# Moving conditioning chunks between a decoder's seams and its dense stages, and regrouping the norm sums

## The reference, cut to what matters

```
m = (silu(c) @ cond_w + cond_b).reshape(c.shape[0], N_COND, 1, D_MODEL)   # cond_w: 1024 x 9216 a layer
def pre(i, h):  return rmsnorm(h, norm_pre[i]) * (1.0 + m[:, 3 * i + 1]) + m[:, 3 * i]
def post(i, h, y, rw): return h + rw * m[:, 3 * i + 2] * rmsnorm(y, norm_post[i])
x = post(0, x, swiglu(pre(0, x), ffn_w_in[0], ffn_w_out[0]), 0.5)
x = post(1, x, mixer(pre(1, x), ...), 1.0)
x = post(2, x, swiglu(pre(2, x), ffn_w_in[1], ffn_w_out[1]), 0.5)
```

## Time and profile before

| what | value |
|---|---|
| runs | 1388.15, 1389.68, 1395.26 us, median 1389.68 |
| profiled execution | 1388.44 us, span 1386.7 us |
| granted TensorE clock, mean | 0.988 |
| TensorE busy | 1327.9 us, 96% of the span |
| VectorE, ScalarE, GpSimd busy | 58%, 42%, 5% |
| DMA | 324.49 MB, mean 234 GB/s |

### The profile page before, as it was taken

One profiled execution on the slowest core, in us unless ns is written; L12 is line 12 of the kernel. 1 busy time (PEld: TensorE's weight loads), 2 busy tenths in 40 slices (PEclk: granted clock), 3 DMA queues, 4 the chain that ended last, 5 costly groups with the idle time before them and its releaser, 6 DMA issues.

```text
span 1386.7 us, 34431 instructions
## 1 busy us (share of the span) xinstructions
PE 1327.9 (96%) x13990; PEld 1268.5 (91%) x13990; DVE 805.6 (58%) x1178; ACT 586.7 (42%) x965; POOL 64.6 (5%) x141
## 2 busy tenths in 40 slices
PE   6899999999989999999999999999998998999997
PEld 5899999999966899999989999998997687999997
DVE  2555553668894655554465555446789657555544
ACT  2532333443565543333363333345337555333442
POOL 4000000110020000000000000002001000000000
PEclk9999999999999999999999999999999999999999
DMA  9878779789989895568876557987997993655552
GB/s 330 262 231 258 218 243 311 224 252 335 293 257 343 266 312 152 155 179 270 261 232 173 157 167 224 291 259 213 315 333 209 331 325 92 171 163 160 145 161 84
DMA packets 423815, 324.49 MB, mean 234 GB/s; under 512 B 15559, under 2 KB 351719, under 8 KB 423696
## 3 DMA queue, kind: packets, MB, share of 16 engines
q1 hardware_dynamic: 421124, 317.03, 75.3%
q0 software_dynamic: 2272, 5.61, 1.3%
q10 hardware_dynamic: 300, 0.13, 0.0%
HBM read 317.93 MB, written 4.78 MB: 233 GB/s over the span
## 4 chain that ended last, share of the span: by engine, by line
PE 87%; DVE 5%; DMA 3%; SPq 2%; ACT 1%; DVEq 1%; issue 1%; POOL 0%; ACTq 0%
PE PS L604 24%; PE PS L605 23%; PE PS L606 23%; PE PS L632 4%; PE PS L666 2%; PE PS L910 2%; PE PS L667 2%; PE PS L668 2%; PE PS L956 1%; SPq L486 1%; DMA direct<-in_cache_sb_v 1%; DMA raw<-in_ffn_w_in 1%; SPq L453 1%; DVE sm L2000 1%; PE PS L676 1%
## 5 line engine op out<-in xcount | busy, mean ns | idle before, releaser
L1702 DVE TENSOR_TENSOR w_lo<-raw,w_hi 128x1024 fp32r<-128x1024 f32 (+1 forms) x368 | 392.9, 1106 | 446.8 <-ACT w_hi L1315 446.3
L1315 ACT ACTIVATE w_hi<-raw 128x1024 fp32r<-128x1024 f32 (+1 forms) x368 | 337.7, 960 | 657.1 <-PE PS L606 576.5
L604 PE MATMUL PS<-a_hi,w_hi 128*128 128x288 f32 x1760 | 524.1, 298 | 0.4 <-issue 0.4
L605 PE MATMUL PS<-a_lo,w_hi 128*128 128x288 f32 x1760 | 519.2, 295 | 0.0
L606 PE MATMUL PS<-a_hi,w_lo 128*128 128x288 f32 x1760 | 517.5, 294 | 0.0
L604 PEld LDWEIGHTS PS<-a_hi,w_hi 128*128 128x128 f32 x1760 | 329.8, 187 | 3.8 <-issue 3.5
L606 PEld LDWEIGHTS PS<-a_hi,w_lo 128*128 128x128 f32 x1760 | 331.4, 188 | 0.0
L605 PEld LDWEIGHTS PS<-a_lo,w_hi 128*128 128x128 f32 x1760 | 330.4, 188 | 0.7 <-issue 0.5
L605 PE MATMUL PS<-h_lo,w_hi 128*128 128x288 f32 x704 | 208.4, 296 | 0.0
L604 PE MATMUL PS<-h_hi,w_hi 128*128 128x288 f32 x704 | 208.1, 296 | 0.0
L606 PE MATMUL PS<-h_hi,w_lo 128*128 128x288 f32 x704 | 208.0, 296 | 0.0
(11 more groups left out here) (324 smaller groups left out, 1159.4 us busy)
## 6 DMA issues: line engine op xcount, KB each, us to landing
raw<-in_ffn_w_in SPq DMA_DIRECT2D x176, 512.0 KB, 5.0
direct<-in_cond_w SPq DMA_DIRECT2D x240, 256.0 KB, 5.0
direct<-in_cache_sb_k SPq DMA_DIRECT2D x128, 256.0 KB, 4.3
direct<-in_cache_sb_v SPq DMA_DIRECT2D x128, 256.0 KB, 4.6
raw<-in_ffn_w_out SPq DMA_DIRECT2D x64, 384.0 KB, 3.8
raw<-in_mix_w_in SPq DMA_DIRECT2D x48, 512.0 KB, 7.1
raw<-in_ffn_w_out SPq DMA_DIRECT2D x64, 320.0 KB, 4.5
side<-in_cond_w SPq DMA_DIRECT2D x48, 256.0 KB, 5.3
```

The costliest lines, as they stand in the source:

```text
L604: pe.matmul(out, whi, hi, start=begins and i == 0, stop=False)
L605: pe.matmul(out, whi, lo, start=False, stop=False)
L1315: act.activation(w_hi[:, s, at_:at_ + n], raw[:, s, at_:at_ + n], ACT.Copy)\
L1702: tt(w_lo[:, s, at_:at_ + n], raw[:, s, at_:at_ + n], w_hi[:, s, at_:at_ + n], ALU.subtract).then_inc(lo_done.sem, 1)
```

## The change

Five edits, and the DMAs that belong to them:

- In `group(1)` of the first feed-forward's output part, TensorE does all four chunks of third 0 behind output step 5, where it did two.
- SyncE loads slots 2 and 3 of third 2 inside the output part (`i == 2`, next to output steps 10 and 11) and no longer between the mixer's input loads.
- `mixer_seam` holds eight chunks, where it held ten; the sums of pairs 1 to 3 stand in one run, then a chunk, then `spread_x` and two chunks, where it was three.
- `layer_seam` puts a chunk ahead of pair 0, one behind it, the sums of pairs 1 to 3 in one run, a chunk, then `spread_x`.
- The third seam of layer 0 ends with two chunks (numbers 4 and 5), where it was three (4 to 6); chunk 6 goes ahead of chunks 7 to 9 behind input step 2 of the second feed-forward.

```diff
--- before.py
+++ after.py
@@ -515,7 +515,7 @@
                             if l + n and s == 2:
                                 sp.wait_ge(ss_out.sem, ss_out.at(l + n, 0) * 32)
                             cond_side(lc, x, s)
-                        if i == 2 and s < 2 and n == 0:
+                        if i == 2 and s < 4 and n == 0:
                             cond_part(lc, x, 2, s)
                         if i == 2 and s >= 2:
                             sp.wait_ge(w_used.sem, w_used.at(l, POS_IN[n] + N_IN))
@@ -553,8 +553,6 @@
                         mix(l, mix_w_in, POS_MI, j, j % 2, MIX_STEPS[j][1])
 
                 mix_in(0, 1)
-                for s in range(2, 4):
-                    cond_part(l, 2, 2, s)
                 mix_in(2, 3)
                 key_chunks(l, 0, 1)
                 mix_in(4)
@@ -747,7 +745,7 @@
                             for slot in (2, 3):
                                 part_chunk(l, 1, 2, slot)
                         elif s % 3 == 2 and n == 1 and not final:
-                            for c in ((7, 8, 9), (10, 11))[s // 3]:
+                            for c in ((6, 7, 8, 9), (10, 11))[s // 3]:
                                 cond_chunk(l, *cond_in, *divmod(c, 4))
                     with pe.Fori(3, NCH // 2 + 3) as i:
                         for s in range(2):
@@ -774,15 +772,15 @@
                         if first and s == 1:
                             pe.wait_ge(h_ready.sem, h_ready.at(l, (n + 1) * N_IN))
                         out_chunk(l, n, i * 4 + s, s)
-                        if s < chunks and s % 2 == 1:
+                        if chunks and s == 1:
                             pe.wait_ge(mod_ready.sem, mod_ready.at(l, 1))
-                            for slot in (s - 1, s):
+                            for slot in range(chunks):
                                 part_chunk(l, 2, 0, slot)
 
                 NG = N_OUT // 4
                 group(0, True)
                 if n == 0:
-                    group(1, chunks=2)
+                    group(1, chunks=4)
                 with pe.Fori(2 if n == 0 else 1, NG - 1) as i:
                     group(i)
                 group(NG - 1)
@@ -817,20 +815,17 @@
 
             def mixer_seam(l):
 
-                part_chunk(l, 2, 0, 2)
+                side_chunk(l, 2, 0)
                 spread_y(l, 0)
-                part_chunk(l, 2, 0, 3)
-                side_chunk(l, 2, 0)
-                side_chunk(l, 2, 1)
+                for slot in range(1, 4):
+                    side_chunk(l, 2, slot)
                 pair_squares(l, 0, 0)
-                side_chunk(l, 2, 2)
-                pair_squares(l, 0, 1)
-                side_chunk(l, 2, 3)
-                pair_squares(l, 0, 2)
                 part_chunk(l, 2, 2, 0)
-                pair_squares(l, 0, 3)
+                for j in range(1, KP):
+                    pair_squares(l, 0, j)
+                part_chunk(l, 2, 2, 1)
                 spread_x(l, 1)
-                for slot in range(1, 4):
+                for slot in range(2, 4):
                     part_chunk(l, 2, 2, slot)
 
             def layer_seam(l):
@@ -840,10 +835,12 @@
                 spread_y(l, 2)
                 for slot in range(1, 4):
                     part_chunk(l + 1, 1, 0, slot)
-                for j in range(KP - 1):
+                side_chunk(l + 1, 1, 0)
+                pair_squares(l, 2, 0)
+                side_chunk(l + 1, 1, 1)
+                for j in range(1, KP):
                     pair_squares(l, 2, j)
-                    side_chunk(l + 1, 1, j)
-                pair_squares(l, 2, KP - 1)
+                side_chunk(l + 1, 1, 2)
                 spread_x(l + 1, 0)
                 side_chunk(l + 1, 1, 3)
                 for slot in range(2):
@@ -1281,7 +1278,7 @@
                 for h in range(2):
                     last = column_sums(5, ysq[:, 2 * ((N_MO - 1) % 2) + h, :], False, h == 1)
                 last.then_inc(ssy_done.sem, 1)
-                filled_seam(l, 1, 2, DP_C[0], 0, 4 if l + 1 < L else 1, 7 if l + 1 < L else 4, l)
+                filled_seam(l, 1, 2, DP_C[0], 0, 4 if l + 1 < L else 1, 6 if l + 1 < L else 4, l)
                 ffn(l, 1, (2, DP_C[0]))
                 if l + 1 < L:
                     layer_seam(l)
```

## The result

The changed kernel takes 1402.83 us (median of 6 runs, 1399.27 to 1407.84); the kernel before, beside it on the same chip, takes 1389.59. The ratio is 1.0098, with a 95% interval of 1.0076 to 1.0119: slower by 13 us. The forecast was 1393.0 with a range up to 1400, so the time is outside the range.

What follows compares the result with a forecast made beforehand. It took one long TensorE stream (87% of the chain) as the bound. Seams -7.5, chunks +4.70, stalls +6.8 gave +4.0 on 1388.44, so 1392.4; half of 1.24 added gave 1393.0, own range 1389 to 1396.5, wider range 1386 to 1400.

Steps and rivals of the forecast that it cites:

- The stall before step 12: First feed-forward's output part: two early chunk loads delay step 12's weights, TensorE stands 3.4 us per layer, 6.8 in all.
- The clock behind the stall: Rival: stalls at output step 12 bring half-clock products, 1.6 to 3 us per layer, giving 1396.2 to 1399; chance 0.20.
- the wait of 2.59 in the third seam: Layer 0's third seam: chunk waits 2.59 for its DMA, next step takes usual time; cited against the lowered-clock rival.
- The standstill of layer 0's mixer seam: The 1.47 standstill behind the spread would come ahead of it, unhidden; bounds 0 and 1.47, 0.50 taken.
- DMA is quieter there now, and I take 0.50: Layer 0's mixer seam: reason given for costing the standstill ahead of the spread at 0.50.
- The layer seam: Seam between the layers: 0.97 from sums in one run and 0.18 from fewer chunks, less 0.55 for its standstill.
- ends when something arrives, whatever I reorder: Layer seam: standstill ends at 719.54 regardless of order; bounds 0 and 1.15, 0.55 taken.
- the third seam: Layer 0's third seam: fewer chunks behind the spread cut its distance to the next step from 12.48 to 10.75, 1.73.
- layer 1's mixer seam: Sums in one run give 1.33 and fewer chunks behind the spread 2.65.
- the chunks: Chunks moved to dense stages: two more behind output step 5 per layer, chunk 6 behind input step 2; 4.70 added.
- the reload behind chunk 6: Second feed-forward: later slot reload delays input step 5's weights some 4 us; costed at nothing, 1 to 2 if uncovered.
- The floor of 10.75 from spread to next step: Seams: third input pair ready 7.51 behind the spread, plus half a step of 3.24; nothing gets below 10.75.

Runs made afterwards that it cites:

- late_loads: Changed kernel with the loads of third 2's slots 2 and 3 issued behind the weights of output steps 12 and 13; 1390.66 us, ratio 1.0013.
- stall_filled: Changed kernel plus 64 matmuls with unused sums, turned over four column groups, ahead of output step 12; 1399.54 us, ratio 1.0074.
- one_load: Changed kernel with slot 2's load kept early and slot 3's moved behind step 12's weights; 1396.71 us, ratio 1.0049, runs 1390.1 to 1398.32.
- late_pad: late_loads plus 40 full-width matmuls added at TensorE's start, before the first products; 1402.03 us, one run.
- late_shift: late_loads plus 80 matmuls into one group of 32 columns ahead of the first products; 1401.98 us, ratio 1.0083.
- late_fill160: late_loads plus 80 matmuls (160 in the trace) over four column groups ahead of the first products; 1387.78 us, ratio 0.9990.
- nine_fill80: nine_chunks plus 40 matmuls (80 in the trace) over four column groups ahead of the first products; 1385.98 us, ratio 0.9979.
- nine_chunks: Changed kernel with three chunks behind output step 5, nine in the mixer seam, slot 2's load behind step 12's weights, slot 3's at its old place; 1387.70 us, ratio 0.9986.

## Why the prediction was wrong

**The stall before step 12: right, with a margin misread.** The step "the weights of step 12 land 6.1 later, 0.86 to spare, 1.88 given by the chunks: 3.4 us" measured 3.20 and 4.21. In late_loads, with those bytes elsewhere, it was 0; with half of them 0.55 to 0.85. The margin was smaller than 0.86: the row at 249.66 is the split of step 13, which waits for step 11's last product, and in the trace of the kernel before step 12 itself begins at 249.47.

```profile
249.47 0.29 PE L604 MATMUL PS<-h_hi,w_hi 128*128 128x288 f32 x1
```

The low half was ready at 248.80, so 0.67 is left. In layer 1 the same split begins at 917.35 and step 12 at 918.97; with 0.96 for the split that leaves 0.66. So the margin does not tell the layers apart. The weights do: counted from the start of the output part, their split begins 5.6 later in layer 0 and 6.6 in layer 1, on both sides of the 6.1, and from issue to split they take 8.2 and 9.4, where both took 7.4 to 7.6 before. Why they took 1.2 longer in layer 1 is not shown.

**The clock behind the stall: the step that failed.** The forecast's sum has no term for it. It stood among the rivals with 0.20 and in the forecast at nothing, because the wait of 2.59 in the third seam was followed by a step of the usual length. It came in both layers. The price was 1.6 each, the low end of the rival's 1.6 to 3. stall_filled shows that it is the idle time that brings it: the same late weights, TensorE busy, whole clock. One wait without a loss was no proof against it. 0.55 to 0.85 (one_load) cost no clock, 3.20 and 4.21 did, but between them the length alone does not decide: the clock stayed at 1.00 behind the wait of 2.59 in the kernel before and behind the standstill of 2.14 in the changed one, and fell behind the 2.00 in the earlier trace rows and, in late_loads, behind the 1.43 that ends at 947.80:

```profile
948.00:950.00 2.00, 2.00 (x72) 2.00 (x68) 1.01 (x1) 0.08 (x1) 2.00 (x4) 0.55 0.17 19
```

What else decides there no run shows. With the two half clocks the forecast would have been 1396.2, still 6.6 short.

**The standstill of layer 0's mixer seam: right place, wrong size, and a second one.** The prediction said that it would come ahead of the spread, at the same place in the program. It did, 79 records from the seam's end before and after; and the place 128 records ahead of it, at 207, where the kernel before shows no gap, now has one too. The term that was mis-sized, and its reason, is "DMA is quieter there now, and I take 0.50": the two lasted 2.14 and 1.06. The windows around the first one show that there was no DMA traffic to speak of:

```profile
281.00:283.00 2.00, 0.35 (x13) 0.08 (x1) 1.93 (x3) 1.91 (x4) 1.42 (x2) 1.00 0.00 0
283.00:285.00 2.00, 1.50 (x67) 1.50 (x70) 1.91 (x4) 1.42 (x3) 0.35 (x1) 1.00 0.00 0
```

A DMA share of 0.00 and a standstill of 2.14: the length does not come from contention. The seam cost 0.77 where 1.21 was to be gained, a miss of 2.0. late_pad, late_shift and late_fill160 show that the places go by the count of instructions. In their profiles the three seams take 2.0 to 2.9 less than in late_loads, and in nine_fill80's 2.4 less than in nine_chunks; the times of late_fill160 and nine_fill80 lean the same way, with overlapping intervals.

**What the standstills are.** The last DMA traffic ahead of the standstill of 2.14 is one packet of 16 KB on the queue that the profile calls instruction; it starts at 280.88, 2.62 before TensorE goes on at 283.50. The DMA view of the changed kernel from 280.75 to 281:

```profile
q8 instruction: 1, 0.02, 28.3%
```

The 17 traces hold 70 standstills of 0.35 or more that the profile puts down to "issue", and 68 of them end 2.2 to 2.9 after the start of such a packet, whether DMA moves 398 GB/s meanwhile or nothing. (The other two, of 0.42 and 0.38, lie in the mixer.) So TensorE goes on some 2.5 after the packet starts, and a standstill is as long as TensorE has run out of work before that: with the 2.14 the packet started 0.48 before TensorE stopped, with the 1.06 it was 1.29. That explains a 2.14 with DMA idle. What makes a packet start sooner or later is not shown, and no run changed the fetching itself.

The Trainium skill (Runtime: NRT & Kernel Launch, Instruction fetch mechanics) says that instructions are fetched in blocks ahead of need. The period of 128 matmuls with their weight loads, 256 instructions, that moved exactly with the added matmuls speaks for it, as do the packets; the standstills are then this fetch, and not something else, as the prediction had it. By the rule the fetch is mostly hidden; the runs show 0.4 to 2.6 us a time where TensorE works off 256 small instructions in 3.7 us. In the products, where 256 take 128 x 0.133 = 17 us, it is hidden but for one gap of 0.35 to 0.90 in each of seven runs.

**The layer seam: mis-sized.** 0.14 instead of 0.60. Squares to spread fell to 4.68, as forecast, but the standstill grew from 0.93 to 1.53 and ended 8.96 behind the first squares where it had ended 9.08 behind them. The forecast had named this case ("ends when something arrives, whatever I reorder") and bounded its price by 1.15; it took 0.55, and it was 1.01.

**Right within 0.4:** the third seam (1.64 for 1.73), layer 1's mixer seam (3.60 for 3.98, spread 4.66 behind the squares), the chunks (4.7 for 4.70), and no wait for the reload behind chunk 6. The floor of 10.75 from spread to next step was 0.1 to 0.3 too low (10.84 in the third seam, 11.09 in the mixer seams).

**What stays open.** The seams come to -4.6 for the forecast's -7.5, the chunks to +4.7, the stalls to +7.4 for 6.8, the clock to +3.2 for 0: +10.7 of the 12.6 between the spans and the 13.2 between the medians. So the clock is 3.2 of what the forecast missed, the seams 2.9, the stalls 0.6, in sum 6.7 of 9.8. In the spans the start adds 2.4 and the rest takes 0.5 off; whether the medians have more of something else is not settled. Nor is when a packet of instructions starts, or one_load's spread.

## What to carry to other kernels

A load that is moved in a queue is paid for by what stands behind it: compare the margin of the next transfer that somebody waits for (here 0.67 us) with the bytes put ahead of it (6.1 us), and move the load behind that transfer, which here cost nothing. When a stall like the 3.2 and 4.2 here is forecast for TensorE, add the half-clock products behind it to the sum; if it can't be avoided, put work that has to be done anyway into it. In stretches of many small matmuls count instructions as well as time: a gap that the profile puts down to nothing may sit at a fixed count, and whether an edit helps can hang on where that lies. The profile's DMA view of the 3 us ahead of such a gap tells whether a packet of the instruction queue stands there.

## What the runs showed of the hardware that was not expected

- Small matmuls of 32 stationary columns, turned over the four groups of 32 columns, take 0.029 to 0.031 us each in the trace (3.70 for 128, 4.93 for 160); the same ones all into one group take 0.110 (28.13 for 256, 17.65 for 160). The granted clock was 1.00 in all of them but for the first 0.8 us of the 4.93. It looks as if the four groups work side by side, and one group does not overlap with itself.
- TensorE can stand still at every 256th instruction that falls among small and dense ones, for up to 2.6 us, whether DMA carries 398 GB/s or nothing. It goes on 2.2 to 2.9 us after the start of a 16 KB packet on the instruction queue (68 of 70 cases), so some of these places show no gap.
- A stall of 3.20 or 4.21 brought TensorE's granted clock from 1.00 to 0.53 and 0.50 for some 3 us; stalls of 0.55 to 0.85 did not, and with matmuls in the long stall it stayed at 1.00. In between the length does not decide: 1.43 and 2.00 were followed by half clock, 2.14 and 2.59 were not. The first products of the program, behind an idle time of 5 us, run at 0.50 too, and at 1.00 when that time is filled.
